# Probabilities times values in split fp32r instead of plain fp32, in the windowed attention of a two-layer hybrid encoder

## The reference, cut to what matters

```python
def windowed_gqa(q, k, v, sink, cos, sin):
    q = apply_rope(q, cos, sin)
    k = apply_rope(k, cos, sin)
    # blocks of 128 queries; each sees its own block of keys and the two beside it
    s = jnp.einsum('bnqhgd,bnkhd->bhgqk'...) * (HEAD_DIM ** -0.5)
    s = jnp.where(valid[None, :, None, None], s, -1e30)
    ...
    p = jax.nn.softmax(jnp.concatenate([s, sink_col], axis=-1), axis=-1)[..., :-1]
    o = jnp.einsum('bnhgqk,bnkhd->bnqhgd', p.astype(v.dtype), vw)
    return o.reshape(bsz, seq, A_WIDTH)
```

## Time and profile before

| what | value |
|---|---|
| time, median of 3 runs | 2832.11 us (2832.09 to 2838.44) |
| the profiled execution, its own time | 2832.11 us |
| its span, first to last instruction | 2830.3 us |
| PE busy | 2694.4 us, 95% |
| DVE, ACT, POOL busy | 52%, 40%, 44% |
| mean granted TensorE clock | 0.982 |
| the loop of `win`, layer 0 | about 205 to 400 us of the span |
| the loop of `win`, layer 1 | about 1600 to 1795 us |

### The profile page before, as it was taken

One profiled execution on the slowest core, in us unless ns is written; L12 is line 12 of the kernel. 1 busy time (PEld: TensorE's weight loads), 2 busy tenths in 40 slices (PEclk: granted clock), 3 DMA queues, 4 the chain that ended last, 5 costly groups with the idle time before them and its releaser, 6 DMA issues. The chain is left out here.

```text
span 2830.3 us, 39130 instructions
## 1 busy us (share of the span) xinstructions
PE 2694.4 (95%) x15174; PEld 2154.0 (76%) x15174; DVE 1484.6 (52%) x1837; ACT 1142.3 (40%) x1894; POOL 1246.6 (44%) x1128
## 2 busy tenths in 40 slices
PE   8989999999999999999999999899999999999998
PEld 5867767777778779778767777677777887897787
DVE  5136536777377343475241565377764764335842
ACT  3124434666365414341121344266663653244211
POOL 2474335443365450265434743444433654303753
PEclk9999999999999999999999999999999999999998
DMA  5253224232365555754242532333224564567442
GB/s 203 90 149 105 82 75 136 90 97 68 105 191 186 187 158 155 237 179 131 82 145 89 153 110 70 120 104 97 83 68 134 189 199 161 161 161 262 144 125 104
DMA packets 394072, 380.89 MB, mean 135 GB/s; under 512 B 90144, under 2 KB 332448, under 8 KB 393888
## 3 DMA queue, kind: packets, MB, share of 16 engines
q1 hardware_dynamic: 354912, 296.39, 34.6%
q10 hardware_dynamic: 38976, 82.00, 7.8%
HBM read 248.22 MB, written 130.09 MB: 134 GB/s over the span
## 5 line engine op out<-in xcount | busy, mean ns | idle before, releaser
L266 PE MATMUL pair<-h_hi,w_hi 128*128 128x512 f32 x1792 | 738.7, 412 | 72.9 <-PEq L203 39.0
L266 PE MATMUL pair<-h_hi,w_lo 128*128 128x512 f32 x1792 | 707.8, 395 | 0.0
L266 PE MATMUL pair<-h_lo,w_hi 128*128 128x512 f32 x1792 | 707.6, 395 | 0.0
L246 POOL TENSOR_TENSOR w_hi<-w_stage,masks 128x256 fp32r<-128x256 f32 x312 | 258.1, 859 | 639.6 <-PE pair L266 602.7
L266 PEld LDWEIGHTS pair<-h_hi,w_hi 128*128 128x128 f32 x1792 | 341.8, 191 | 195.0 <-issue 82.5
L266 PEld LDWEIGHTS pair<-h_hi,w_lo 128*128 128x128 f32 x1792 | 341.6, 191 | 75.4
L266 PEld LDWEIGHTS pair<-h_lo,w_hi 128*128 128x128 f32 x1792 | 342.5, 191 | 70.2 <-issue 5.3
L281 ACT ACTIVATE ev<-pair 128x512 f32<-128x512 f32 x224 | 132.9, 593 | 453.8 <-PE pair L266 452.8
L251 POOL TENSOR_TENSOR w_lo<-w_stage,w_hi 128x256 fp32r<-128x256 f32 x312 | 248.5, 828 | 6.1
L1692 POOL TENSOR_TENSOR w_lo<-w_stage,w_hi 128x256 fp32r<-128x256 f32 x128 | 150.6, 1206 | 169.2 <-ACT w_hi L1806 169.2
L1447 ACT ACTIVATE diff_p<-pair,diff_stat 128x1024 f32<-128x1024 f32 x128 | 143.1, 1118 | 126.1 <-DVE diff_stat L1550 122.2
(11 more groups left out here) (292 smaller groups left out, 4940.2 us busy)
## 6 DMA issues: line engine op xcount, KB each, us to landing
w_stage<-in_w_in SPq DMA_DIRECT2D x132, 512.0 KB, 4.1
proj<-ev ACTq DMA_DIRECT2D x132, 512.0 KB, 2.7
gate<-proj SPq DMA_DIRECT2D x48, 512.0 KB, 3.6
prep_x<-proj SPq DMA_DIRECT2D x24, 512.0 KB, 4.3
resid<-xT SPq DMA_DIRECT2D x16, 512.0 KB, 5.6
diff_vx<-proj SPq DMA_DIRECT2D x16, 512.0 KB, 3.3
prep_g<-gc_rows SPq DMA_DIRECT2D x16, 512.0 KB, 5.0
qd_t<-prep_eg SPq DMA_DIRECT2D x16, 512.0 KB, 2.6
```

The lines of the kernel that those rows point to most:

```text
L246: last = nc.gpsimd.tensor_tensor(w_hi[s][:, part], w_stage[s][:, part], bcast(ones, PIECE), ALU.mult)
L266: last = nc.tensor.matmul(bank(self.banks[half]), a[s][:, c, :], b[:, c, w], start=(c == 0 and n == 0), stop=(c == KC - 1 and n == 2))
```

## The change

The values and the probabilities are each split into a high and a low fp32r part. `sum_values` runs three fp32r products in place of each plain fp32 one. The values now lie in a zero-padded tile of 5 x 64 columns (zeros, group 0, zeros, group 1, zeros), from which 128 columns are taken such that the 64 real ones fall on the partitions of head 0 or of head 1; both heads add into all 128 partitions of bank 6. The high part of the probabilities is written by ACT where the copy was (`high_part` in place of `keep`), the low part by DVE at the end of each step (`low_part`), from PSUM and the high part. Each part has one buffer where the copy had two. At the start of the phase DVE clears the two value tiles, ACT writes the high values in place of the copy, and DVE writes the low values ahead of `low(1)`. `turn(n)` and `sum_values` wait for the low part where they waited for the copy; `scores(0)` and `scores(1)` wait for the low values.

```diff
-                V = sb("win_v", [P, NT, 2 * HD])
-                v_turned = pairs[0][:].rearrange("p a (t s) -> p (a t) s", s=P)
+                v_hi, v_lo = sb("win_v_hi", [P, NT, 5 * HD], F32R), sb("win_v_lo", [P, NT, 5 * HD], F32R)
+                both = lambda v: v[:].rearrange("p t (b d) -> p t b d", d=HD)[:, :, 1:4:2, :]
+                v_turned = pairs[0][:].rearrange("p a (t b d) -> p (a t) b d", b=2, d=HD)
...
-                PT = [sb(f"win_p{j}", [P, 3, 2, 2 * P]) for j in range(2)]
+                p_hi, p_lo = (sb(f"win_p_{n}", [P, 3, 2, 2 * P], F32R) for n in ("hi", "lo"))
...
                         if n < 2:
-                            pe.wait_ge(q["v_tok"], START + 1)
+                            pe.wait_ge(q["v_lo"], START + 1)
...
                         pe.wait_ge(q["probs"], START + n + 1)
                         if n:
-                            pe.wait_ge(q["p_kept"], START + n)
+                            pe.wait_ge(q["p_lo"], START + n)
...
-                        pe.wait_ge(q["p_kept"], START + 2 * j + 2)
+                        pe.wait_ge(q["p_lo"], START + 2 * j + 2)
                         if j:
                             pe.wait_ge(q["gated"], START + j)
                         for b in range(nb):
-                            for h in range(2):
-                                last = nc.tensor.matmul(bank(6)[h * HD:(h + 1) * HD, 0:2 * P],
-                                                        V[:, first + b, g * HD:(g + 1) * HD], PT[j % 2][:, b, h, :],
-                                                        start=b == 0, stop=b == nb - 1)
+                            for c, (a, p) in enumerate(((v_hi, p_hi), (v_hi, p_lo), (v_lo, p_hi))):
+                                for h in range(2):
+                                    at = (1 + 2 * g - h) * HD
+                                    last = nc.tensor.matmul(bank(6)[:, 0:2 * P], a[:, first + b, at:at + P], p[:, b, h, :],
+                                                            start=(b == 0 and c == 0 and h == 0),
+                                                            stop=(b == nb - 1 and c == 2 and h == 1))
...
-                    def keep(n):
+                    def high_part(n):
                         _, _, nb, _ = window(n)
                         act.wait_ge(q["turned"], START + n + 1)
-                        if n % 2 == 0 and n >= 4:
-                            act.wait_ge(q["summed"], START + n // 2 - 1)
-                        nc.scalar.activation(of_block(PT[n // 2 % 2], n, nb), by_tile(pairs[2], nb), ACT.Copy)\
-                            .then_inc(q["p_kept"], 1)
+                        if n % 2 == 0 and n:
+                            act.wait_ge(q["summed"], START + n // 2)
+                        nc.scalar.activation(of_block(p_hi, n, nb), by_tile(pairs[2], nb), ACT.Copy).then_inc(q["p_hi"], 1)
...
-                    nc.scalar.activation(V[:], v_turned, ACT.Copy).then_inc(q["v_tok"], 1)
+                    act.wait_ge(q["pads"], START + 2)
+                    nc.scalar.activation(both(v_hi), v_turned, ACT.Copy).then_inc(q["v_hi"], 1)
...
+                    def low_part(n):
+                        _, _, nb, _ = window(n)
+                        dve.wait_ge(q["p_hi"], START + n + 1)
+                        nc.vector.tensor_tensor(of_block(p_lo, n, nb), by_tile(pairs[2], nb),
+                                                of_block(p_hi, n, nb).bitcast(F32), ALU.subtract).then_inc(q["p_lo"], 1)
+
+                    for v in (v_hi, v_lo):
+                        nc.vector.memset(v[:].bitcast(F32), 0.0).then_inc(q["pads"], 1)
                     cosine(0)
                     rotate(0)
                     low(0)
                     cosine(1)
                     rotate(1)
+                    dve.wait_ge(q["v_hi"], START + 1)
+                    nc.vector.tensor_tensor(both(v_lo), v_turned, both(v_hi).bitcast(F32), ALU.subtract)\
+                        .then_inc(q["v_lo"], 1)
                     low(1)
...
                         if n % 2 and n >= 3:
                             gate_output((n - 3) // 2)
+                        if n:
+                            low_part(n - 1)
+                    low_part(STEPS - 1)
                     gate_output(QUADS - 1)
```

More of the change, by code:

```diff
@@ L138, in build_program @@
         AHEAD["win"] = SIDE_AHEAD_IN
-        SIGNALS["win"] = (["sink_in", "sink_set", "x_in0", "x_in1", "x_in2", "cosined", "sined",
-            "rotated", "hi", "lo", "v_in", "v_turned", "v_tok", "z_in0", "z_in1", "tanh", "z_gate",
-            "scored", "masked", "negmax", "exped", "recip", "probs", "turned", "p_kept", "summed",
+        SIGNALS["win"] = (["sink_in", "pads", "sink_set", "x_in0", "x_in1", "x_in2", "cosined", "sined",
+            "rotated", "hi", "lo", "v_in", "v_turned", "v_hi", "v_lo", "z_in0", "z_in1", "tanh", "z_gate",
+            "scored", "masked", "negmax", "exped", "recip", "probs", "turned", "p_hi", "p_lo", "summed",
             "gated", "stored"] + SIDE)
@@ L1047, in _ @@
                         if n:
-                            keep(n - 1)
+                            high_part(n - 1)
                     side_out(tail_half(0))
-                    keep(STEPS - 1)
+                    high_part(STEPS - 1)
                     side_out(tail_half(1))
```

## The result

| | before | after |
|---|---|---|
| time, median | 2833.3 us (2832.09 to 2838.44, 4 runs) | 2853.03 us (2849.86 to 2854.64, 4 runs) |
| ratio | | 1.0068, 95% interval 1.0056 to 1.0082 |
| span of the profiled execution | 2830.3 us | 2849.7 us |

The change makes the kernel 0.68% slower; the medians lie 19.7 us apart. The forecast was 2860 us with a range of 2846 to 2873, and slower with a chance of 0.94.

A forecast was written before the change was run, and what follows sets the result against it. PE was taken to bound the kernel, busy 95% of the span and 194.05 of 195 us in the loop. 2832.1 + 15.4 (PE's work) + 12.2 (new waits) = 2859.7, called 2860 us, range 2846 to 2873.

The forecast's parts named there:

- PE's own work: Sums of the windowed loop: 18 fp32r matmuls add 0.55 us per three-block sum, 0.27 per two-block sum; +15.4 us in all.
- The new wait: Shared steps: the low part delays DVE's mask and ACT's side-half eviction, so PE waits; 6.1 us a layer, +12.2 in both.
- Steps 6, 22 and 26: Shared three-block steps: mask 1.09 us late, eviction ends at 265.82, next side matmul on PE waits 0.93 us.
- DVE's step 9 is not the later one: Before step 10's low part: DVE's step 9 would end near 0.9 us, so ACT's copy, ending at 0.92, sets the start.
- Step 14: Shared two-block step: delay of 1.24 us against 0.49 us of room, a new PE wait of 0.64 us.
- Step 18: Shared step where PE already waits 0.95 us for ACT: it takes the full delay, 1.1 us more.
- DVE busy but not short: Windowed loop: the low part's busy time, some 29 us a layer, is covered; DVE goes from 109 to about 137 of 195 us.
- The start of the phase: Clears and low values fall into DVE's idle time, and high values replace a copy of the same size; free.
- Faster, because plain fp32 is dearer: Rival at the sums: plain fp32 takes four passes, fp32r one, 24 against 18; 19 us less, 2813 us, chance 0.03.
- The clock: Rival: PE's clock halves after step 18's 2.05 us wait, +3 us (2863); after the new waits too, 2884 us; chance 0.06.
- The sum: Whole kernel: 2832.1 + 15.4 + 12.2 = 2859.7, called as 2860 us.

## Why the prediction was right, point by point

*PE's own work, +15.4.* Right. Measured +14.2 with the sums alone. The distance of 0.1195 us, taken from the other attention, came out as 0.118; the sum of 18 took 2.12 us for 2.15. The new group also enters 0.23 us behind the last side matmul (258.43 to 258.66), where the old one took 0.32 (257.30 to 257.62), which the forecast had reckoned with.

*The new wait, +12.2.* The path was right at six of the seven places and in part at the seventh; the size was too high, 9.0 us of idle time and 9.8 from start to start. By place:

- Steps 6, 22 and 26, forecast 0.93 each: the low part runs from 0.95 to 1.91 us as forecast, but the mask starts at 1.82, ahead of its recorded end, and not at 1.93. The waits were 0.86, 0.85 and 0.75.
- Step 10, forecast 0.93 as well. "DVE's step 9 is not the later one" was wrong in layer 0: its last operation ended at 1.26 us and not near 0.9, 0.3 us behind ACT's copy. The low part started at 1.18 and the wait was 0.96. In layer 1 the two ended within 0.1 us of each other, and it was 0.76. That the wait of layer 0 came out so near the forecast is two misses that cancel.
- Step 14, forecast 0.64, measured 0.45. The mask was 1.17 us late for 1.24, and the eviction starts 0.10 us ahead of the recorded end of what stands before it.
- Step 30, for which I took over the 0.64 of step 14: 0.21. It has no later step's sink to set (`set_sink`), so its eviction starts at 4.27 us and not at 4.50.
- Step 18, forecast 1.1 more than before, measured 0.55 more. This term was sized wrong: the low part that stands ahead of its mask belongs to step 17, which has two key blocks. It is 512 columns wide and takes 0.69 us, so the mask starts 0.55 us late (1.38 for 0.83), and the eviction 0.54. The forecast had looked at this for step 14, and not for step 18:

```profile
315.82 0.69 DVE L1092 TENSOR_TENSOR win_p_lo<-pair,win_p_hi 128x512 fp32r<-128x512 f32 x1
```

*DVE busy but not short.* Right for one low part: moving it or the eviction removed part or all of the waits at the same load. It stops being right at two.

*The start of the phase, free.* Right: 1.0003 with the values' split alone.

*Faster, because plain fp32 is dearer.* Wrong here, and for the reason given: the pairing of the halves, worth 1.3 us per three-block sum (2.74 against 1.45). The Trainium skill (FP8 and Floating Point Precision, TensorE Precision Notes) gives true fp32 four passes. The trace agrees on one half: 256 columns at 2.4 GHz are 0.107 us, 6 x 4 x 0.107 is 2.56 us, and 2.74 were measured. The Trainium skill (TensorEngine Tiling, Key Properties) has different tiles run matmuls in parallel, and by 1.45 against 2.74 us the trace agrees with that too.

*The clock.* It didn't fall behind the 1.50 us at step 18; I had put 2.05 us there. In the loop with the doubled low part it fell behind every wait of 1.84 us and more.

*The sum.* The loops alone are 23.9 us longer. The profiled execution is 19.4 us longer, so the stages that the change doesn't touch took 4.4 us less in it. No term of the forecast has this, so of the 27.6 us forecast 19.7 came: 3.7 us were sized too dear in the loops, and the rest is missing here. That is not the chance of one execution: in all six versions with fp32r sums the median rose by less than the loops (by 1.5 to 4.2 us), in the five others that keep plain fp32 sums by more (0.3 to 2.9). In the profiles the time outside the two loop stretches is 2374 to 2380 us for the six versions with fp32r sums and 2379 to 2386 us for the six with plain ones. The granted clock accounts for a good part: outside the loops the traces' record of it has 95.2 us at half clock before and 82.4 after, and half of that difference is 6.4 us; over the versions it is 88 us on average with fp32r sums and 94 with plain ones, which is 2.9 of the 5.1 us between their mean times. Why the clock falls less in stages that are the same instructions is open; the executions of the kernel before spread from 2827.1 to 2840.0 us by themselves, and no run isolates it.

## What to carry to other kernels

Before you trade plain fp32 matmuls for split fp32r ones, look whether the plain ones run in pairs on two halves of the array: count how many start in their stretch, don't multiply the passes. Where an operation is added at the end of an engine's step, ask what stands behind it in the next step and follow that to the engine that bounds the kernel; an operation of up to 0.96 us a step, on an engine that is busy little more than half the time, cost 9 to 10 us here, through an eviction that had stood behind the exponentials with 0.2 us of room. And when a wait appears, look first for work that is ready early and stands behind work that is late: moving the eviction took no work away and gave all of it back, and the old wait of 0.95 us with it. And when you size the operation for a step, take the size of the step that it belongs to, which may be the one before.

## What I had not expected of the hardware

- Matmuls on different halves of the array don't have to be neighbours. With six instructions on one half followed by six on the other, the second row set in beside the third instruction of the first, so the sum took 1.93 us and not 2.74.
- In the loops of these runs each wait of PE of 1.84 us and more (five in each layer with the low part doubled) was followed by 3.4 us at 1.2 GHz, worth another 1.7 us by estimate; waits up to 1.75 us (low part alone, step 19) were not. The length of the wait doesn't settle it everywhere: at the start of the phase in layer 1, waits of 2.03 to 2.08 us were not followed by it in four of the twelve profiles, while eight waits of 2.00 to 2.34 us in the others were.
